# Two norms between the blocks summed in one pass over X and closed as columns, with VectorE taking every tap of three convolution tiles

## What is computed

```python
# end of the first block: attention output, gated, added; then its final norm
x = x + gate * y
x = _rmsnorm(x, final_norm_g)                  # norm 1
# start of the second block
h = rmsnorm(x, norm_mix_g_2[0])                # norm 2, of the result of norm 1
p = h @ w_in_ab_2[0]                           # 512 columns "a", 1024 columns "b" (v and gate)
ya = fnet_heads(p[..., :512], fnet_map)        # DFT over tokens and head, then a map
u = v * sigmoid(gate)                          # v, gate: 512 channels each
u = depthwise_conv(u, conv_w, 31 taps) + conv_b
u = silu(layernorm(u per head of 128, ln_g, ln_b))
x = x + concatenate([ya, u]) @ w_out_ab_2[0]
# then a swiglu feed-forward, a pooling mixer, a second feed-forward, and the last norm
```

## Time and profile before

| what | value |
|---|---|
| time, median of 3 runs | 754.55 us (753.44 to 757.85) |
| profiled execution | 755.56 us, span 753.8 us |
| granted TensorE clock, mean | 0.991 of full speed |
| TensorE matmul busy | 721.7 us (96%) |
| VectorE busy | 503.9 us (67%) |
| ScalarE busy | 389.9 us (52%) |

### The profile page before, as it was taken

How to read it: one execution, slowest core, us unless ns; L and a number is a source line. 1 busy time by engine, 2 the same in 40 slices (tenths; PEclk the granted TensorE clock), 3 DMA queues, 4 the chain that set the end, 5 groups by cost and what they waited for, 6 DMA issues and landing times.

```text
span 753.8 us, 9658 instructions
## 1 busy us (share of the span) xinstructions
PE 721.7 (96%) x3900; PEld 629.7 (84%) x3900; DVE 503.9 (67%) x760; ACT 389.9 (52%) x602; POOL 2.4 (0%) x8
## 2 busy tenths in 40 slices
PE   3999995999999999999999999999999999999996
PEld 2888885999999999888888888888888888888885
DVE  4866987986976789987664454555576554454444
ACT  4146526347675667846844434444466533434423
POOL 0000000000000000000000000000000000000000
PEclk9999998999999999999999999999999999999998
DMA  9999774796934434234364555545324455545201
GB/s 348 418 420 422 324 270 177 296 423 272 400 124 169 167 130 184 79 113 168 142 249 171 200 187 184 206 168 196 139 113 171 181 206 171 203 184 179 102 0 57
DMA packets 23085, 156.65 MB, mean 208 GB/s; under 512 B 2560, under 2 KB 2688, under 8 KB 5120
## 3 DMA queue, kind: packets, MB, share of 16 engines
q1 hardware_dynamic: 22464, 153.41, 53.6%
q0 software_dynamic: 576, 2.62, 1.0%
HBM read 154.97 MB, written 1.05 MB: 207 GB/s over the span
## 4 chain that ended last, share of the span: by engine, by line
PE 77%; DVE 10%; ACT 8%; DMA 3%; issue 1%; SPq 0%; DVEq 0%; ACTq 0%
PE pb L1454 19%; PE pb L1456 18%; PE pb L1455 18%; PE pb L1524 13%; DVE w L956 4%; PE pb L1683 2%; DVE raw L959 2%; DMA raw<-w_dram 2%; ACT w L593 2%; PE pb L1784 1%; ACT r L698 1%; ACT t L701 1%; PE pb L1530 1%; DVE rs L1015 1%; PE pb L1714 1%
## 5 line engine op out<-in xcount | busy, mean ns | idle before, releaser
L956 DVE TENSOR_TENSOR w<-raw,w 128x2048 fp32r<-128x2048 f32 x97 | 221.4, 2291 | 142.6 <-ACT w L593 142.5
L593 ACT ACTIVATE w<-raw 128x2048 fp32r<-128x2048 f32 x97 | 184.8, 1913 | 157.2 <-PE pb L1456 114.9
L1454 PE MATMUL pb<-w,r 128*128 128x512 f32 (+1 forms) x640 | 244.2, 381 | 0.7 <-DVE r L959 0.3
L1456 PE MATMUL pb<-w,r 128*128 128x512 f32 (+1 forms) x640 | 241.0, 377 | 0.0
L1455 PE MATMUL pb<-w,r 128*128 128x512 f32 (+1 forms) x640 | 240.6, 376 | 0.0
L1454 PEld LDWEIGHTS pb<-w,r 128*128 128x128 f32 x640 | 120.5, 188 | 23.1 <-issue 1.8
L1456 PEld LDWEIGHTS pb<-w,r 128*128 128x128 f32 x640 | 120.4, 188 | 22.5
L1455 PEld LDWEIGHTS pb<-w,r 128*128 128x128 f32 x640 | 120.6, 188 | 21.2
L1454 PE MATMUL pb<-r,w 128*128 128x256 f32 x352 | 101.6, 289 | 7.1 <-DVE r L956 6.6
L1455 PE MATMUL pb<-r,w 128*128 128x256 f32 x352 | 100.2, 285 | 0.0
L1456 PE MATMUL pb<-r,w 128*128 128x256 f32 x352 | 100.1, 284 | 0.0
(11 more groups left out here) (174 smaller groups left out, 572.0 us busy)
## 6 DMA issues: line engine op xcount, KB each, us to landing
raw<-w_dram SPq DMA_DIRECT2D x129, 1024.0 KB, 4.9
ow<-w_dram SPq DMA_DIRECT2D x8, 1024.0 KB, 19.2
ow<-w_dram SPq DMA_DIRECT2D x8, 512.0 KB, 15.6
oh<-w_dram SPq DMA_DIRECT2D x2, 1024.0 KB, 21.5
x<-x_dram SPq DMA_DIRECT2D x2, 512.0 KB, 6.0
f<-rc_dram POOLq DMA_DIRECT2D x1, 1024.0 KB, 5.1
acc<-row_dram POOLq DMA_DIRECT2D x2, 512.0 KB, 5.4
out_dram<-f SPq DMA_DIRECT2D x4, 256.0 KB, 2.3
```

The lines of the kernel that those rows point to most:

```text
L593: return e.activation(out, in_, ACT.Copy, **kw)
L956: return e.tensor_tensor(out, a, b, op)
L1454: e.matmul(out, a_hi, b_hi, start=start, stop=False)
L1456: return e.matmul(out, a_lo, b_hi, start=False, stop=stop)
```

## The change

Norm 2's sum is the sum of squares of `x * g * r1`, with r1 norm 1's factor of the token; so r1 comes out of the sum and both sums can be taken from X before it is scaled. What is done:

1. `two_squares` and `two_adds` take the place of `square` and `add` in the `ao` projection: for each tile two squares (plain, and scaled by `final_norm_g`) and two sums, `NA[0]` and `NA[1]`. The second pass over X goes.
2. `two_sums` makes four one-column matmuls after three `kt` of the first `b` pair; the two norms are then closed on columns of two elements (two roots, two reciprocals, three products), and `two_rows` after six `kt` turns them into rows with `spread`, a matmul of a broadcast column with the identity. ScalarE copies both rows from PSUM at once.
3. MATS[22] is split at `d == 6` of the projection, before the last two `ao` tiles are taken up; before, it came after all eight.
4. After the first `b` pair the order on ScalarE and VectorE is a new one: MATS[24] before the sigmoids, MATS[25] after the gates 2 and 3 on both engines, MATS[26] and [27] after 20 more taps, MATS[29] in the middle of the layer norm.
5. VectorE does all 31 taps of tiles 0, 1 and 2. Tile 2's 12 matmuls, their diagonals and the final add go.
6. The layer norm's variance is summed as two one-column matmuls for each tile, its root and reciprocal are of 128x2, and `ln_row` spreads them as a row into PSUM. Its tiles come in the order 3, 0, 1, 2, and its steps stand between groups `both(kt)`, the mixed products of one `kt`, in the order 0, 1, 2, 3, 7, 4, then 5 and 6.
7. The identity is fetched by a DMA of its own at the kernel's start, after `vec` and before `c`; its semaphore `s_id` has no wait.

```diff
-NPE = 12
-LN = (0, 1, 3, 2)
+LN = (3, 0, 1, 2)
 # SyncE
             e.dma_start(vec[:, :], vec_d).then_inc(s_vec, 16)
+            e.dma_start(cst[:, 0:P], cst_d[:, 0:P]).then_inc(s_id, 16)
             e.dma_start(acc[0][:, :], c_d).then_inc(s_c, 16)
...
 # ScalarE
+            def two_squares(d):
+                for m in range(2):
+                    n = 2 * (d - 1) + m
+                    if n >= NT:
+                        p.wait_ge(s_na, 7 + n - NT + 1)
+                    to = tt[n % NT] if d else NA[m]
+                    kw = {"scale": V("final_norm_g", d)} if m else {}
+                    e.activation(to[:, :], X[:, d, :], ACT.Square, **kw).then_inc(s_sq, 1)
...
                 if d == 4:
                     fill(18)
+                if d == 6:
+                    fill(19)
                 p.wait_ge(s_x2, d + 1)
-                square(2, d)
                 raw_high(0, R2, d, gg[:, d:d + 1])
-            fill(19)
-            row_root(2)
-            col_root(0, rcol[:, 0:2])
+                two_squares(d)
+            sums = bank_of("ns", 0)[:, 0:4]
+            p.wait_ge(*ended("ns", 0))
+            e.activation(rcol[:, 0:2], sums[:, 0:2], ACT.Sqrt, ...).then_inc(s_rtc, 1)
+            p.wait_ge(s_col, 2)
+            e.activation(rcol[:, 2:4], rcol[:, 2:4], ACT.Sqrt, ...).then_inc(s_rtc, 1)
             fill(20)
...
+            p.wait_ge(*ended("rb", 0))
+            copy(RSt[:, :, :], bank_of("rb", 0)[:, :]...).then_inc(s_rsb, 1)
+            for b in range(4):
+                p.wait_ge(*ended("b", b))
+                copy(F1[:, 6 + b if b < 2 else 2 + b, :], out_of("b", b)).then_inc(s_b, 1)
             fill(21)
-            row_root(3)
-            col_root(1, rcol[:, 2:4])
-            fill(22)
             gated(0)
             gated(1)
-            gated(2)
-            gated(3)
             start_tap(0)
             start_tap(1)
+            gated(2)
+            gated(3)
+            start_tap(2)
+            fill(22)
...
+            diagonals(*range(6, 16))
             fill(25)
+            diagonals(*range(16, 31))
...
+            fill(26)
+            for d in (3, 0, 1):
+                ln_square(d)
+            for d in (3, 0, 1):
+                ln_root(d)
+            for d in (3, 0, 1):
+                ln_high(d)
+            ln_square(2)
+            ln_root(2)
+            ln_high(2)
             fill(27)
 # VectorE
+            def two_adds(d):
+                for m in range(2):
+                    n = 2 * (d - 1) + m
+                    p.wait_ge(s_sq, 16 + 2 * d + m + 1)
+                    if n >= 2:
+                        p.wait_ge(s_na, 7 + n - 1)
+                    tt_(NA[m][:, :], NA[m][:, :], tt[n % NT][:, :], ADD).then_inc(s_na, 1)
...
-            project("ao", 2, ..., {4: MATS[21]})
-            fill(19)
+            project("ao", ..., two_adds, {4: MATS[21], 6: MATS[22]})
...
+            tt_(rcol[:, 4:6], rcol[:, 0:2], rcol[:, 2:4], MUL).then_inc(s_col, 1)
             fill(20)
+            p.wait_ge(s_rsb, 1)
             for d in range(8):
                 stt(X[:, d, :], X[:, d, :], V("final_norm_g", d), RS[0][:, :], MUL, MUL)...
-                if d >= 2:
-                    add(3, d - 1)
...
             for d in range(2):
                 gated(d, ...)
+            fill(21)
+            pump(16)
             for d in range(2, 4):
                 gated(d, ...)
             fill(22)
-            pump(12)
...
+            pump(20)
+            fill(24)
+            pump(20)
             for h in range(4):
                 p.wait_ge(s_fhi, h + 1)
                 low(R1, h, out_of("fm", h), s_flo)
-                pump(2)
+                pump(3)
+            fill(25)
+            pump(85 - tap_n["n"])
...
+            ln_centre(3)
+            pump(4)
+            ln_centre(0)
+            ln_centre(1)
+            pump(4)
+            for d in (3, 0, 1):
+                ln_inverse(d)
+            fill(26)
+            ln_scale(3)
+            ln_centre(2)
+            ln_scale(0)
+            ln_scale(1)
+            ln_low(3)
+            ln_inverse(2)
+            ln_low(0)
+            ln_low(1)
+            ln_scale(2)
+            ln_low(2)
             fill(27)
 # TensorE
+            def spread(out, col):
+                return e.matmul(out, col.broadcast_to([P, P]), ident, start=True, stop=True)
...
+            def two_sums():
+                bank_free("ns", 0)
+                p.wait_ge(s_na, 7 + 14)
+                for m in range(2):
+                    for a in range(2):
+                        done = e.matmul(..., NA[m][:, a * P:a * P + P], ones_sb[:, 0:1], start=True, stop=True)
+                done.then_inc(s_ps, 1)
+            def two_rows():
+                bank_free("rb", 0)
+                p.wait_ge(s_col, 3)
+                for i, c in ((0, 0), (1, 4)):
+                    for a in range(2):
+                        o = i * T + a * P
+                        done = spread(bank_of("rb", 0)[:, o:o + P], rcol[:, c + a:c + a + 1])
+                done.then_inc(s_ps, 1)
-            head(20, run("b", 0, 1, 2, 3), 0, lambda: close(2, 0))
-            head(22, run("b", 4, 5, 6, 7), 0, lambda: close(3, 1))
+            pair(20, first, R2, s_rlo, 0, range(3), last=False)
+            two_sums()
+            pair(20, first, R2, s_rlo, 0, range(3, 6), first=False, last=False)
+            two_rows()
+            pair(20, first, R2, s_rlo, 0, range(6, 8), first=False)
+            pair(22, run("b", 4, 5, 6, 7), R2, s_rlo, 0, range(8))
...
+            both(0)
+            ln_var(3)
+            ln_mean(0, ...)
+            ln_mean(1, ...)
+            both(1)
+            ln_var(0)
+            ln_var(1)
+            ln_row(3)
+            both(2)
+            ln_mean(2, ...)
+            ln_row(0)
+            ln_row(1)
+            both(3)
+            ln_var(2)
+            both(7)
+            ln_row(2)
+            both(4)
             for a in range(2):
                 for c in range(2):
                     if a and c:
                         turn(0, 0)
-                    for kt in range(4, 8):
+                    for kt in (5, 6):
                         mixed(kt, c, a)
```

More of the change, by code:

```diff
@@ L350, in two_block_program @@
         root = sb("root", [P, T])
-        RS = [sb(f"rs{i}", [P, T]) for i in range(2)]
+        RSt = sb("rs", [P, 2, T])
+        RS = [RSt[:, i, :] for i in range(2)]
         NA = [sb(f"na{i}", [P, T]) for i in range(2)]
@@ L498, in freed @@
                 return s_rt, ROWS_AT[i]
[L499 to L500 removed]
+            if kind == "ns":
+                return s_col, 1
+            if kind == "rb":
+                return s_rsb, 1
             if kind == "u":
@@ L690, in _ @@
                 p.wait_ge(s_x1, d + 1)
-                square(1, d)
+                square(d)
             row_root(1)
@@ L804, in _, with diagonals @@
             start_tap(1)
-            def diagonals(d, js):
-                for j in js:
[L808 to L815, removed]
+            gated(2)
+            gated(3)
+            start_tap(2)
+            fill(22)
+            def diagonals(*js):
+                for j in js:
+                    if j >= 8:
+                        p.wait_ge(s_dgm, j - 7)
+                    copy(dg[j % 8], ident, scale=V("conv_w_2", 4 * j + 3)).then_inc(s_dg, 1)
             p.wait_ge(s_cst, 16)
@@ L831, in _ @@
                 if h < 3:
-                    diagonals(2, range(2 * h, 2 * h + 2))
-            start_tap(2)
+                    diagonals(2 * h, 2 * h + 1)
             for h in range(4):
@@ L1125, in _, with project @@
                     y_tile(d)
-            def project(kind, i, done, scale, before, raw_, streams):
+            def project(kind, done, scale, before, raw_, add_, streams):
                 for d in range(8):
@@ L1688, in ln_mean, with ln_row @@
                 p.wait_ge(*sums)
-                e.matmul(PB[OUT.bank["ln", d]][:, 0:T], ones, F1[:, d, :], start=True, stop=True).then_inc(s_lnm, 1)
+                e.matmul(bank_of("ln", d)[:, 0:T], ones, F1[:, d, :], start=True, stop=True).then_inc(s_lnm, 1)
             def ln_var(d):
                 p.wait_ge(s_lnq, LN.index(d) + 1)
-                e.matmul(PB[OUT.bank["ln", d]][:, 256:512], ones, tt[d][:, :], start=True,
-                         stop=True).then_inc(s_lnv, 1)
-            convolved(2, NPE, range(NPE))
-            convolved(3, 31, range(0, 20))
-            ln_mean(0, (s_tap, tap_at[0, 30]))
-            ln_mean(1, (s_tap, tap_at[1, 30]))
-            convolved(3, 31, range(20, 31))
+                for a in range(2):
+                    done = e.matmul(bank_of("ln", d)[:, T + a:T + a + 1], tt[d][:, a * P:a * P + P], ones_sb[:, 0:1],
+                                    start=True, stop=True)
+                done.then_inc(s_lnv, 1)
+            def ln_row(d):
+                p.wait_ge(s_lni, LN.index(d) + 1)
+                for a in range(2):
```

(28 more changed lines are left out.)

234 lines of the change are left out of this document (88 added, 146 removed).

## The result

The changed kernel takes 777.07 us (median of four runs, 775.88 to 777.09), the kernel before 755.85 us (753.44 to 757.85): 2.67% slower, by the recorded ratio of 1.0267 with a 95% interval of 1.024 to 1.0295. The profiled execution has a span of 774.1 us, 20.3 more than the 753.8 of before.

What follows compares the result with a forecast made beforehand. TensorE was taken to set the end, VectorE without slack in the convolution. Terms 0.45 - 4.2 + 6.0 + 1.3 + 3.0 + 1.8 gave +8.4 us: 764.0 profiled, 763.0 forecast, slower by 1.1%, range 757.0 to 766.0.

Steps and rivals of the forecast that it cites:

- TensorE's work: Changed stretch: 7.78 us of matmuls removed, 4.89 added with spreads and returns from fp32, net 2.9 us less.
- old waits gone: TensorE's two waits, for split weights (0.37) and a layer norm square (0.87), go: counted as 1.3 us less.
- start: Kernel start: the identity's DMA issued ahead of `c` costs one issue slot, 0.45 us, between 0 and 0.6.
- adds late: Sums between the blocks: `two_sums` waits for all 14 adds on VectorE, 6.0 us, between 4.6 and 6.5.
- clock after it: After the wait for the adds, some 14 matmuls run at 1.2 GHz: 1.3 us more, bounds 0 and 1.3.
- MATS[25] late: Before the third `a` tile: TensorE waits 3.0 us for the split of MATS[25]; lower bound 1.0.
- VectorE in the convolution: nothing: Convolution: VectorE gets 12 taps (4.8 us), taps 0 and 1 end some 3 us before `ln_mean(0)`; cost nothing.
- X turned back: Transposes of X: MATS[30] and [31] split after `ln_high(2)`, VectorE's copies come late, 1.8 us; bounds 0 and 2.3.
- column chain between sums and rows: Roots, reciprocals and products between `two_sums` and `two_rows` need some 1.8 us, hidden behind three `kt`, 4.3 us.
- price of a spread: One matmul of a broadcast column with the identity taken at 0.224 us, bounds 0.185 and 0.432.
- drain at a table switch: ScalarE: by the skill page a switch costs 2.66 us, not 1.28, making X turned back 1.4 us dearer; not in the sum.
- slower by over 0.5%: Whole kernel: case that the change is slower by more than 0.5%, given chance 0.77.

Runs made afterwards that it cites:

- e8_later: e7_turn with the one-column sums after four `kt` instead of three and the rows after seven instead of six: 753.61 us, ratio 0.9967 to the kernel before.
- e9_before_id: The kernel before with only the identity's DMA added at the start, after `vec` and ahead of `c`: 758.25 us, ratio 1.0017 to the kernel before.
- e2_slab22: The changed kernel with the split of MATS[22] put back behind the last `ao` tile: 769.71 us, ratio 1.017 to the kernel before.
- e5_warm: The changed kernel with 48 unread matmuls put before the wait for the 14 adds: 773.54 us, ratio 1.0203 to the kernel before.
- e4_slab25: The changed kernel with MATS[25] split before the gates of tiles 2 and 3 on ScalarE and VectorE: 774.44 us, ratio 1.0244 to the kernel before.
- e1_bank: The changed kernel with three PSUM bank numbers skipped, so tile 3's convolution gets its old bank: 766.7 us, ratio 1.0137 to the kernel before.
- e7_turn: e6_all with MATS[30] split before the last tile's silu on ScalarE and before its scaling on VectorE: 756.82 us, ratio 1.0003 to the kernel before.
- e3_ident: The changed kernel without the identity's DMA at the start, the whole constant tile fetched later: 773.17 us, ratio 1.0211 to the kernel before.
- e6_all: The changed kernel with the edits of e1_bank, e2_slab22, e3_ident and e4_slab25 together: 758.24 us, ratio 1.0021 to the kernel before.

## Why the prediction was wrong

The sign was right and the size less than half. Point by point, in profiled time against profiled time (+20.3):

| step of the prediction | forecast | measured | how |
|---|---|---|---|
| TensorE's work | -2.9 | about -2.9 | e8_later, 3.1 less for 3.3 worked out |
| old waits gone | -1.3 | -1.2 | waits after |
| start | +0.45 | +2.4 in the profile (0.9 at the first matmul), 1.3 by e9_before_id | TensorE is through with the third `kt` at 265.41 against 263.01 |
| adds late | +6.0 | +6.00 | e2_slab22 |
| clock after it | +1.3 | +2.9 | e5_warm, 8.22 against 5.31 |
| MATS[25] late | +3.0 | +2.83 | e4_slab25 |
| "VectorE in the convolution: nothing" | 0 | +5.1, and 2.9 of clock | e1_bank |
| X turned back | +1.8 | +1.76 | e7_turn |
| sum | +8.4 | about +19.8 | |

**The step that failed** is the one that cost the convolution at nothing. It asked whether VectorE's taps would be done in time, and they were: e1_bank removes the wait with every tap where it was. It did not ask what else the first convolution matmul waits for. Two things were in sight: the change takes names out of a list from which PSUM banks are dealt in turn, and the convolution's bank is a fixed number. With them the list gives `fm` tile 2 as the former tenant, and VectorE's order (20 taps, two splits, 20 taps, then the lows) gives its release at 326.8. That is 5.1 us, and 2.9 for the lower clock behind it, 8 of the 12 us that the forecast was short.

**Mis-sized** were the clock and the start. For the clock the pace was right (0.21 against 0.12), its length too short: in the trace of before TensorE had been at half clock for some 3 us of work after it took up work again, from 125.53 to 128.65, here 5 to 7. For the start the issue slot was counted and not that `c` would also take longer to land behind 128 small rows (4.24 to 5.08 us in six profiles, 3.50 to 4.14 in six without them), nor what the clock may do behind a later start.

**Right** were the three waits that came out of following the orders of ScalarE and VectorE row by row, to 0.2 us each, and that the column chain between sums and rows is hidden. The price of a spread was right too: the eight pieces of `two_rows` take 1.05 us, (1.05-0.27)/7x2 = 0.22 each. The 1.4 us that the prediction named for a drain at a table switch are not seen; measured is the load alone. Here ScalarE goes from the copy to the load to the sigmoid with no time between them:

```profile
283.87 1.90 ACT L599 ACTIVATE w<-raw 128x2048 fp32r<-128x2048 f32 x1
285.80 1.28 ACT L794 ACT_TABLE_LOAD   x1
287.09 0.42 ACT L794 ACTIVATE t<-t 128x256 f32<-128x256 f32 x1
```

Two slips of arithmetic changed nothing: 0.41-0.24 is 0.17 and not 0.18, and the chances add up to 0.76 and not 0.77 for slower by over 0.5%.

**Left open.** e1_bank and e3_ident gave 2 to 3 us more than their own waits and the clock behind them add up to. In their profiles this lies ahead of the sums, where the granted clock was 1.00 and the changed kernel's 0.73. Why the clock falls in one execution and not in the next of the same code, and whether the medians carry the same share, no run here shows.

## What to carry to other kernels

When a change takes a buffer out of a ring, ask of every later user of the ring who has it before, above all of users with a fixed number; the wait that comes of it carries the name of an engine that nobody thought of. Where TensorE sets the end, price a wait with the clock that may fall behind it, here up to 3 us for waits of 1.7 us and more. And where a split of 2.2 us stands in the engines' order decided three of the four new waits. With the splits in other places, the banks and the start as before and the sums one `kt` later, the same arithmetic gave 0.3% instead of taking 2.7%.

## What the runs showed of the hardware

- A wait of 1.69 us (e6_all) or 2.83 us (e1_bank) can bring the clock to 1.2 GHz for several microseconds of work, or not: it stayed at 1.00 after 1.69 us in e7_turn, after 2.83 in the changed kernel's profile, and after 3.63 in e3_ident's. After every wait of 5.1 to 6.4 us it fell, in all twelve profiles. The time of one kernel then goes with its mean clock: e7_turn from 752.14 at 0.991 to 759.08 at 0.985. The kernel before does so too, from its one wait of 6.4 us and its start: of its 29 runs beside e6_all, 17 lie between 753.75 and 756.05 at 0.991 or 0.992, 12 between 756.82 and 758.48 at 0.988 or 0.989. That its spread comes from these two places is argued, not shown.
- Keeping the engine at work in a wait with 48 matmuls that nobody reads kept the clock at 1.00 (e5_warm), 2.9 us for nothing but the writing.
- Behind a DMA of 64 KB in 128 rows of 512 bytes, one of 512 KB took 4.24 to 5.08 us to land in six profiles, against 3.50 to 4.14 in six without it, beside its issue slot of 0.45.
